# Three small reorderings inside the state-space and latent-attention layers of a two-block decoder

## The reference, cut to what matters

```
h = rms_norm(x); proj = h @ w_in                       # z | xbc | dt | q_a | kv_a | k_rope
xbc = silu(conv4(xbc)); dt = softplus(dt_raw + dt_bias)
a = dt * -exp(a_log);  y = ssd_scan(xs * dt, a, B, C) + xs * d_skip
y = rms_norm(y * silu(z))  per group of 512
q = rms_norm(q_a) @ w_q_b ; kv = rms_norm(kv_a) @ w_kv_b   # 8 heads, 128 + 64 wide
q, k = rms_norm over the 192 of a head, rotated in the last 64
o = causal softmax attention(q, k, v)
x = x + concat(y, o) @ w_out
x = x + cross attention to mem ;  x = x + swiglu(x)
```

## Time and profile before

| | us |
|---|---|
| median of 3 runs | 3523.42 (3523.11 to 3524.86) |
| the profiled execution, device time | 3520.93 |
| its span | 3519.1 |
| PE busy | 3456.8 (98%) |
| DVE busy | 2107.8 (60%) |
| ACT busy | 1717.3 (49%) |
| DMA, mean rate | 179 GB/s |

### The profile page before, as it was taken

The page is one execution under the profiler, slowest core; times in us unless marked ns, Lnnn a source line. Parts: engine busy times, 40 slices in busy tenths (PEclk is TensorE's granted clock), DMA queues, the critical chain, the costliest instruction groups (busy, mean ns, idle before and its releaser), DMA issues.

```text
span 3519.1 us, 43525 instructions
## 1 busy us (share of the span) xinstructions
PE 3456.8 (98%) x18590; PEld 2968.8 (84%) x18590; DVE 2107.8 (60%) x2188; ACT 1717.3 (49%) x2024; POOL 22.7 (1%) x42
## 2 busy tenths in 40 slices
PE   7999999999999999999999999999999999999999
PEld 6888888888888888888888888888898888888887
DVE  6766667554656866655545545577666555555454
ACT  4743464356555465554434434445755644344343
POOL 1000000000000000000000000000000000000000
PEclk9999999999999999999999999999999999999999
DMA  6554554554555444445555555554445455555554
GB/s 236 197 178 142 194 199 163 198 183 168 193 178 183 174 147 153 166 146 180 191 191 191 191 192 190 185 175 171 150 144 180 144 192 189 194 186 188 194 188 167
DMA packets 88578, 630.91 MB, mean 179 GB/s; under 512 B 10064, under 2 KB 10304, under 8 KB 13248
## 3 DMA queue, kind: packets, MB, share of 16 engines
q1 hardware_dynamic: 85104, 611.75, 50.4%
q0 software_dynamic: 3280, 16.36, 1.3%
HBM read 625.98 MB, written 2.10 MB: 178 GB/s over the span
## 4 chain that ended last, share of the span: by engine, by line
PE 81%; DVE 9%; ACT 5%; DMA 3%; issue 1%; DVEq 0%; POOL 0%; ACTq 0%; POOLq 0%
PE G L547 25%; PE G L549 12%; PE G L539 12%; PE G L541 12%; PE G L540 12%; DVE w_lo L459 4%; ACT w_hi L451 3%; DMA w_raw<-in_s_gate 1%; PE G L531 1%; PE G L532 1%; PE G L533 1%; PE M L825 1%; DVE arena L769 1%; PE M L1153 1%; DMA w_raw<-in_s_ssd 1%
## 5 line engine op out<-in xcount | busy, mean ns | idle before, releaser
L459 DVE TENSOR_TENSOR w_lo<-w_raw,w_hi 128x2048 fp32r<-128x2048 f32 (+1 forms) x585 | 1327.7, 2272 | 1220.0 <-ACT w_hi L451 1219.4
L451 ACT ACTIVATE w_hi<-w_raw 128x2048 fp32r<-128x2048 f32 (+1 forms) x585 | 1110.8, 1899 | 1558.1 <-PE G L549 701.4
L547 PE MATMUL G<-x_halves,w_hi 128*128 128x512 f32 x4256 | 1345.2, 397 | 20.1 <-DVE w_lo L459 16.3
L549 PEld LDWEIGHTS G<-x_halves,w_lo 128*128 128x128 f32 x4256 | 801.0, 188 | 186.2
L549 PE MATMUL G<-x_halves,w_lo 128*128 128x256 f32 x4256 | 841.4, 279 | 0.0
L547 PEld LDWEIGHTS G<-x_halves,w_hi 128*128 128x128 f32 x4256 | 650.2, 189 | 24.9 <-issue 14.6
L539 PE MATMUL G<-w_hi,y_halves 128*128 128x512 f32 x1648 | 649.2, 394 | 6.1 <-DVE y_halves L1128 2.6
L541 PE MATMUL G<-w_hi,y_halves 128*128 128x512 f32 x1648 | 642.9, 390 | 0.0
L540 PE MATMUL G<-w_lo,y_halves 128*128 128x512 f32 x1648 | 642.5, 390 | 0.0
L539 PEld LDWEIGHTS G<-w_hi,y_halves 128*128 128x128 f32 x1648 | 309.8, 188 | 70.9 <-DVE y_halves L1128 4.4
L541 PEld LDWEIGHTS G<-w_hi,y_halves 128*128 128x128 f32 x1648 | 309.6, 188 | 64.8
(11 more groups left out here) (445 smaller groups left out, 2686.3 us busy)
## 6 DMA issues: line engine op xcount, KB each, us to landing
w_raw<-in_s_up SPq DMA_DIRECT2D x176, 1024.0 KB, 4.9
w_raw<-in_s_down SPq DMA_DIRECT2D x88, 1024.0 KB, 4.9
w_raw<-in_s_ssd SPq DMA_DIRECT2D x40, 1024.0 KB, 4.9
w_raw<-in_s_hgrn SPq DMA_DIRECT2D x32, 1024.0 KB, 4.9
w_raw<-in_s_gate SPq DMA_DIRECT2D x32, 1024.0 KB, 4.9
w_raw<-in_s_mlstm SPq DMA_DIRECT2D x32, 1024.0 KB, 4.9
w_raw<-in_s_mlstm_gate SPq DMA_DIRECT2D x32, 1024.0 KB, 4.8
w_raw<-in_s_lru SPq DMA_DIRECT2D x16, 1024.0 KB, 5.1
```

Source lines behind the costliest of these rows:

```text
L451: act.activation(whi[p % SETS][:, 0:n_], raw[p % RAW][:, 0:n_], ACT.Copy).then_inc(S("hi_ready"), 1)
L459: dve.tensor_tensor(wlo[p % SETS][:, 0:n_], raw[p % RAW][:, 0:n_], whi[p % SETS][:, 0:n_].bitcast(F32), ALU.subtract).then_inc(S("lo_ready ...
L547: pe.matmul(o, hi[:, k, f], x2, start=first, stop=False, skip_group_check=True)
L549: mm = pe.matmul(o[:, 0:T], lo[:, k, f], x2[:, 0:T], start=False, stop=last, skip_group_check=True)
```

## The change

Three edits, all in the second block's layers.

1. `times_dt` moves from index 15 to index 14, behind `softplus`.
2. The last chunk of the gate z (pieces 32 and 33) is moved out of PSUM by ACT and DVE in front of the split of piece 36 instead of behind it. For the chunk "rows", which has one piece and already did so, nothing changes.
3. All nope keys are scaled by DVE, in two instructions of 128 x 1024, and ACT's eight instructions are gone; PE waits for one semaphore in place of two.

```diff
+        def in_front(name, c):
+            return c.kind == "rows" or c is plans.get(name)[-1] and name[0] == "z"
...
         # act_gemm, for piece j of chunk c
-                    if c.kind == "rows":
+                    if j == c.q - 1 and in_front(name, c):
                         evac_act(act, name, c)
                     split_hi(act, c.p + j + SETS)
                     then(act, c.p + j)
-                if c.kind != "rows" and name[:3] != "ple":
+                if not in_front(name, c) and name[:3] != "ple":
                     evac_act(act, name, c)
...
         # dve_gemm, likewise
-                    if c.kind == "rows":
+                    if j == c.q - 1 and in_front(name, c):
                         evac_dve(dve, name, c)
                     split_lo(dve, c.p + j + SETS)
...
         # mla_pe, step(0)
-                    pe.wait_ge(S("la_k"), l + 1)
-                    pe.wait_ge(S("la_k_second"), l + 1)
+                    pe.wait_ge(S("la_k"), 2 * l + 2)
...
         # mla_act
-            def scale_k():
-                act.wait_ge(S("la_rk"), l + 1)
-                for h in range(8):
-                    o = la["k"][:, 0, h, :]
-                    ins = act.activation(o, o, ACT.Copy, scale=rk_nope[:, 0, h:h + 1])
-                ins.then_inc(S("la_k"), 1)
-            layer_at(act, l, 32, scale_k)
...
         # ssd_dve
-            layer_at(dve, l, 15, times_dt)
+            layer_at(dve, l, 14, times_dt)
...
         # mla_dve
-            def key_second():
-                k = la["k"][:, 1, :, :]
+            def key_nope():
                 dve.wait_ge(S("la_rk"), l + 1)
-                dve.tensor_tensor(k, k, rk_nope[:, 1, :].unsqueeze(2).to_broadcast([P, 8, P]), ALU.mult
-                                  ).then_inc(S("la_k_second"), 1)
+                for t in range(NT):
+                    k = la["k"][:, t, :, :]
+                    dve.tensor_tensor(k, k, rk_nope[:, t, :].unsqueeze(2).to_broadcast([P, 8, P]), ALU.mult
+                                      ).then_inc(S("la_k"), 1)
-            layer_at(dve, l, 32, key_second)
+            layer_at(dve, l, 32, key_nope)
```

More of the change, by code:

```diff
@@ L789, in dve_gemm @@
                     then(dve, c.p + j)
-                if c.kind != "rows":
+                if not in_front(name, c):
                     evac_dve(dve, name, c)
```

## The result

The changed kernel takes 3517.36 us (median of 22 runs) against 3523.06 of the kernel before (22 runs): a ratio of 0.9984, 95% interval 0.9978 to 0.9990. That is 5.7 us less, where 4.7 were forecast. The interval leaves out 1, so the gain is real, but it is under the 0.2% that the prediction took for what such a measurement can tell.

The account below looks back on a forecast made before the run. PE was taken to bound the kernel, busy 3456.8 of a span of 3519.1 us. Terms of 2.73 and 1.98 us sum to 4.71, taken off a median of 3523.42: 3518.7 us, range 3515.0 to 3523.3.

Parts of the forecast that it names:

- The ceiling: Five PE waits at the places the change touches, together 11.1 us or 0.32% of the time, before any working.
- 2.73 us forecast: PE's wait for times_dt at the state-space scores goes whole: 1.49 us in layer 0, 1.24 in layer 1.
- the brackets: Idle times of PE at the scores, run from modelled matmul ends; they gave 2.43 us, the low end for edit 1.
- 1.98 forecast: At the last gate chunk and keys, z_times(3) and the chain behind it come 0.99 us earlier in each layer.
- the 0.3 expected: At the square sums, PE waits about 0.3 us that it did not wait before.
- the 1.34 a layer: High end for edits 2 and 3: PE's second value piece starts at 1338.86 in place of 1340.20.
- Only the first edit pays: Second key product and the split before z_times(3) hold the z chain where it was; 3520.7 us, chance 0.13.
- More waits shrink: ACT's relief of 2.35 us reaches the later waits and up to 11.4 us go; 3512.0 us, chance 0.07.
- It moves nothing: Stalls are taken up behind by splits that are due anyway; 3523.4 us, chance 0.08.
- The late load: Piece 20's load, issued 2.27 us later, delays splits, columns_in and PE's start; at 11.0 us landing 3528.7 us, chance 0.04.

Follow-up runs that it names:

- the kernel with the late load: The changed kernel with the load of piece 20 of each layer held back by one more split: median 3523.16 us against 3517.36.

## Why the prediction was right

**The ceiling and the places.** The time was won at waits of the earlier trace rows: two lines of 2.4 us are gone and 0.5 is new. PE has the same 18590 instructions (3458.1 us busy against 3456.8).

**Edit 1, 2.73 us forecast, 3.07 in stretch A, 2.9 counted from the split of piece 16.** The product stands directly behind the softplus copy, its successors 2.27 later, L2086 on its old place, as worked out. The term was a little small (1.57 for 1.49, 1.34 for 1.24). About 0.1 a layer is the start of the stalled matmuls: the first pair of scores took 0.70 behind its wait and takes 0.59 now, which the sum had left out.

What the working did not ask is why `times_dt` was late at all, and why less so in layer 1. The load of piece 17 was the releaser: SyncE issues it 1.64 us behind ACT's split of piece 16 in layer 0 and 1.31 in layer 1, which is the 0.3 between the layers, and ACT's split of piece 17 starts 4.8 to 5.1 behind that issue. Edit 1 hides that load, so what it is worth depends on how late the load lands in the kernel without it: 1.30 to 1.57 a layer in the three such profiles. That the sum of 2.73 came so close owes something to the one profile it was read from.

The choice to count from start to start was the better one: the brackets would have made it 2.43. That fits the Trainium skill, "Perfetto Trace Analysis", section "Tensor Engine Instruction (MATMUL, LD_WEIGHTS)", which calls the end of a TensorE instruction estimated: the brackets gave 1.34 and 1.09, the starts 1.49 and 1.24, and 1.57 and 1.34 were won.

**Edits 2 and 3, 1.98 forecast, 2.00 measured.** Every link held: key products of 2.35 together, copy-out right behind, split, `z_times(3)`; a new wait at the square sums, 0.21 by its bracket and 0.37 by starts (10.44 us behind the third ones, against 10.07 where PE does not wait), for the 0.3 expected; L1377 and L531 as long as before. What I did not ask is which of the two edits earns the 2.0. The working had the answer in it: the second key product is a link of DVE's chain, ACT's eight were none. Edit 2 alone wins 1.62, edit 3 alone 0.22, both together 1.00. Nor were the 1.34 a layer that the prediction gave as the high end a bound of the place: edit 2 alone is above it.

**The rivals.** "Only the first edit pays" fell with B. "More waits shrink" fell for this change: the waits at step(1) and `z_low(1)` kept their length. That they can go is shown by the kernels with `z_times(3)` first: in the changed kernel that move takes away the wait at step(1), and without edit 3 also most of that at `z_low(1)`. ACT's relief does neither. "It moves nothing" fell: edit 1's gain arrives whole. The late load did not happen (3.57 us of waiting for PE at the split of piece 20); held back, it costs what was said in layer 0. The load that took 11.0 us lies in the first 60 us of the kernel before, not in this stretch: the ten loads issued there took 5.9 at the median, and the DMA engines moved 304 GB/s in the first 42 us (mean of the span 179). The Trainium skill, "DMA: Bandwidth & Descriptors", section "Latency and other measured facts", gives a longer memory latency at high load; whether memory or the shared DMA engines made those loads longer, no run here tells apart.

**The size.** 5.07 us in the stretches against 5.7 in the medians: the difference is inside the interval (3.5 to 7.8 us). The forecast of 4.7 is inside it too. The range of 3515.0 to 3523.3 holds the median.

## What to carry to other kernels

When two edits meet in one chain, work out each alone as well as both: here a relief of 2.35 us on an engine that was not late put 1.13 us of work into the chain of the one that was, and took 0.62 of the 1.62 that the neighbouring edit earns alone. Behind a step that is moved up, look for the first long instruction in front of the next link of the same chain; swapping 0.69 us with 2.29 was worth more than moving the keys. And where an effect is smaller than the scatter of whole executions, compare stretches between two instructions of one profile: here B repeats to 0.01 us, while the times scatter by some 4 to either side. Choose the first of the two so that the engine that bounds the kernel releases it: stretch A started from an instruction that waited for a load and varied by up to 0.4, and started one split earlier it repeats to 0.08 with edit 1.

## What the runs showed of the hardware

TensorE's clock. In the kernel with the late load, PE stood idle for 2.29 us in layer 0 and went on at full clock (1.00, 2.4 GHz). In layer 1 it stood idle for 2.50, and was then granted the lower level (0.50, 1.2 GHz) for some 3 us. Windows of that kernel, layer 0, then layer 1:

```profile
1230.00:1232.00 2.00, 2.00 (x17) 1.81 (x16) 2.00 (x1) 1.60 (x5) 0.00 (x0) 1.00 0.95 401
1232.00:1234.00 2.00, 2.00 (x14) 1.74 (x13) 1.76 (x4) 0.24 (x1) 0.00 (x0) 1.00 0.66 127
```

```profile
2428.00:2430.00 2.00, 0.34 (x3) 0.14 (x1) 2.00 (x4) 1.62 (x2) 0.00 (x0) 1.00 0.00 0
2430.00:2432.00 2.00, 1.16 (x9) 1.04 (x10) 1.83 (x4) 0.72 (x2) 0.00 (x0) 0.71 0.85 266
2432.00:2434.00 2.00, 2.00 (x7) 1.71 (x7) 2.00 (x3) 1.49 (x5) 0.00 (x0) 0.50 0.61 258
2434.00:2436.00 2.00, 2.00 (x12) 1.74 (x12) 0.75 (x2) 0.00 (x0) 0.00 (x0) 0.94 0.93 242
```

In the window at 0.50 PE counts as busy throughout and yet shows 7 matmuls where layer 0 has 14. The third pair of L548 starts 2.03 us behind the end of the wait in layer 0 (1229.85 to 1231.88) and 3.60 in layer 1 (2430.84 to 2434.44): 1.57 more. That closes the account. Counted from the split of piece 16, the way to the third square sums is 2.20 us longer than in the changed kernel in layer 0 and 4.00 in layer 1, 1.80 more, of which 0.21 is the longer wait and 1.57 the clock. (Stretch A shows only 1.4 more, since its start moves with the load of piece 17.) So the fall of the clock nearly doubled what this wait cost, and whether it falls can differ between two layers of one execution.

The lower level also comes behind the wait at 44 us in all nine profiles, one of each kernel. That wait was 2.75 to 5.73 us long. The windows from 42 to 50 us lack 1.7 us of clock in four of the profiles and 3.0 to 3.4 in the other five, and which it is does not follow the length of the wait: 4.83 us in one of the four, 3.34 in one of the five. Over whole executions a lower clock and a longer time go together: of the 22 runs of the changed kernel, the 13 with a mean granted clock of 0.998 or 0.999 took 3513.75 to 3517.92 us, the 9 with 0.997 took 3517.20 to 3521.51. This fits the clock being a part of the scatter; no run isolates it.
